# The first feed-forward layer from its third group on: seven half-size products in place of eight, and the loop's down weights rounded on VectorE

## The reference, cut to what matters

```python
h = rms_norm(x, g_pre_ffn)
f = jnp.square(jax.nn.relu(h @ w_ff1)) @ w_ff2      # 1024 -> 4096 -> 1024
return x + rms_norm(f, g_post_ffn)
```

## Time and profile before

| | |
|---|---|
| median of 3 runs | 1717.76 us (1717.62 to 1719.08) |
| profiled execution | 1716.92 us, span 1715.0 us |
| TensorE busy | 1698.2 us, 99% of the span |
| VectorE busy | 1104.3 us, 64% |
| ScalarE busy | 783.1 us, 46% |
| GpSimd busy | 585.6 us, 34% |
| mean granted TensorE clock | 0.998 |
| DMA | 162.61 MB, mean 95 GB/s |

### The profile page before, as it was taken

One profiled execution on the slowest core, in us unless ns is written; L12 is line 12 of the kernel. 1 busy time (PEld: TensorE's weight loads), 2 busy tenths in 40 slices (PEclk: granted clock), 3 DMA queues, 4 the chain that ended last, 5 costly groups with the idle time before them and its releaser, 6 DMA issues.

```text
span 1715.0 us, 27666 instructions
## 1 busy us (share of the span) xinstructions
PE 1698.2 (99%) x9346; PEld 1459.2 (85%) x9346; DVE 1104.3 (64%) x1973; ACT 783.1 (46%) x1323; POOL 585.6 (34%) x289
## 2 busy tenths in 40 slices
PE   9999999999999999999999999999999999999998
PEld 7877778888888788889999998888888879999997
DVE  5655565333333587688787695566675588688684
ACT  5666543222222433653443354565655453353354
POOL 3232325444445378241210203442523440220221
PEclk9999999999999999999999999999999999999999
DMA  7542213222222242233322333231212233342331
GB/s 197 119 99 85 74 59 126 94 93 96 98 98 87 74 129 87 74 111 99 112 94 90 110 99 111 74 99 49 86 61 74 75 100 96 101 132 74 98 111 50
DMA packets 153712, 162.61 MB, mean 95 GB/s; under 512 B 10627, under 2 KB 114679, under 8 KB 153631
## 3 DMA queue, kind: packets, MB, share of 16 engines
q1 hardware_dynamic: 149167, 158.66, 30.1%
q10 hardware_dynamic: 4464, 2.89, 0.5%
HBM read 157.84 MB, written 3.67 MB: 94 GB/s over the span
## 4 chain that ended last, share of the span: by engine, by line
PE 92%; DVE 4%; ACT 2%; issue 1%; DMA 0%; SPq 0%; DVEq 0%; ACTq 0%
PE ps L1675 49%; PE ps L2080 21%; PE ps L2105 10%; PE ps L1696 2%; PE ps L2187 1%; PE ps L2023 1%; PE ps L1704 1%; PE ps L1894 1%; PE ps L1913 1%; DVE ps L2715 1%; PE ps L1800 0%; PE ps L1806 0%; PE ps L2220 0%; PE ps L1877 0%; DMA lnmult<-const_lnmult 0%
## 5 line engine op out<-in xcount | busy, mean ns | idle before, releaser
L835 POOL TENSOR_TENSOR wlo<-raw,whi 128x1024 fp32r<-128x1024 f32 x92 | 224.8, 2451 | 339.3 <-ACT whi L952 324.0
L1675 PE MATMUL ps<-h_hi,wlo 128*128 128x512 f32 x800 | 323.0, 404 | 6.5 <-DVE gate L2814 5.7
L1675 PE MATMUL ps<-h_hi,whi 128*128 128x512 f32 x800 | 313.1, 391 | 0.0
L1675 PE MATMUL ps<-h_lo,whi 128*128 128x512 f32 x800 | 312.9, 391 | 0.0
L952 ACT ACTIVATE whi<-raw 128x1024 fp32r<-128x1024 f32 x170 | 176.5, 1055 | 251.1 <-PE ps L1675 241.7
L842 POOL TENSOR_TENSOR wlo<-raw,whi 128x1024 fp32r<-128x1024 f32 x60 | 146.9, 2464 | 293.3 <-ACT whi L952 170.2
L1675 PE MATMUL ps<-m_hi,wlo 128*128 128x512 f32 x544 | 214.9, 395 | 0.0
L1675 PE MATMUL ps<-m_hi,whi 128*128 128x512 f32 x544 | 211.9, 390 | 0.0
L1675 PE MATMUL ps<-m_lo,whi 128*128 128x512 f32 x544 | 211.8, 389 | 0.0
L1675 PEld LDWEIGHTS ps<-h_hi,wlo 128*128 128x128 f32 x800 | 150.7, 188 | 38.5 <-issue 8.1
L1675 PEld LDWEIGHTS ps<-h_hi,whi 128*128 128x128 f32 x800 | 150.6, 188 | 33.0
(11 more groups left out here) (411 smaller groups left out, 3938.9 us busy)
## 6 DMA issues: line engine op xcount, KB each, us to landing
raw<-in_ffn_w SPq DMA_DIRECT2D x264, 256.0 KB, 2.9
raw<-in_w_ff SPq DMA_DIRECT2D x128, 256.0 KB, 2.7
raw<-in_hg_w_in SPq DMA_DIRECT2D x64, 256.0 KB, 3.0
raw<-in_w_in SPq DMA_DIRECT2D x40, 256.0 KB, 5.2
raw<-in_cp_w_in SPq DMA_DIRECT2D x24, 256.0 KB, 2.8
raw<-in_w_out SPq DMA_DIRECT2D x16, 256.0 KB, 3.0
raw<-in_cp_w_out SPq DMA_DIRECT2D x16, 256.0 KB, 3.0
raw<-in_hg_w_out SPq DMA_DIRECT2D x16, 256.0 KB, 2.9
```

Of the source, the lines that this page charges most:

```text
L835: pool.tensor_tensor(wlo[:, u % RING, :, :], raw[:, u % RING, :, :], whi[:, u % RING, :, :].bitcast(F32), ALU.subtract).then_inc(unit_lo, 1)
L1675: mm = pe.matmul(ps[:, b, :], wt[:, s, a, m * P:(m + 1) * P], xt[:, kts[a], :], start=starts and a == 0 and i == 0, stop=last)
```

## The change

In the first feed-forward layer, groups 0 and 1 stay as they are. Groups 2 to 7 are done as twelve blocks of 256 columns, each seven products of half size (12 matmuls of 256 columns each). TensorE's order is now up 0, norm, up 1, down 0, down 1, block 0, then five turns of (block, block, down), then block 11 and down 7. The weight sums and the low parts of the forms are VectorE's, as in the gated layers; so are now the low parts of the loop's down weights (`ffn_down_low`), 8 tiles of 128 x 512 a turn. GpSimd does nothing from unit 15 of the layer to unit 60. The four token sums are made once, between up 1 and the first `acc` copies. The buffers `hid` and `hid2` are now `sq` and `ss`. Counters of the later layers are shifted to match. The forms have 11 slots (the gated layers 12).

The core of the diff; on VectorE:

```diff
+            def ffn_token_sums():
+                dve.wait_ge(tokens_made, 4)
+                for k in range(4):
+                    dve.scalar_tensor_tensor(out=f3[:, k, :], in0=xT[:, 4 + k, HALF:], scalar=col("g_pre_ffn", 4 + k),
+                                             in1=f1[:, k, HALF:], op0=ALU.mult, op1=ALU.subtract).then_inc(tokens_made, 1)
+                dve.wait_ge(tokens_made, 8)
+                dve.tensor_tensor(f1[:, :, HALF:], f1[:, :, HALF:], f1[:, :, 0:HALF], ALU.subtract).then_inc(tokens_made, 1)
+                dve.wait_ge(tokens_made, 9)
+                for k in range(4):
+                    dve.scalar_tensor_tensor(out=f2[:, k, :], in0=xT[:, 4 + k, HALF:], scalar=col("g_pre_ffn", 4 + k),
+                                             in1=f1[:, k, HALF:], op0=ALU.mult, op1=ALU.subtract).then_inc(tokens_made, 1)
+                dve.wait_ge(tokens_made, 13)
+                for k in range(4):
+                    dve.scalar_tensor_tensor(out=f1[:, k, 0:HALF], in0=xT[:, 4 + k, 0:HALF], scalar=col("g_pre_ffn", 4 + k),
+                                             in1=f2[:, k, :], op0=ALU.mult, op1=ALU.subtract).then_inc(tokens_made, 1)
...
+            def ffn_hidden(j, t, i=None):
+                dve.tensor_tensor(hid2[:, :], ffn_kept(j)[:, t, :], ffn_kept(j)[:, t, :], ALU.mult).then_inc(hid_ready, 1)
+                dve.wait_ge(hid_hi, at(i, 4, 8 + 2 * j + t + 1))
+                dve.tensor_tensor(m_lo[:, 2 * (j % 2) + t, :], hid2[:, :], m_hi[:, 2 * (j % 2) + t, :].bitcast(F32),
+                                  ALU.subtract).then_inc(hid_lo, 1)
...
+            def ffn_forms(y, i, after):
+                ffn_sum(y, 1, i)
+                ffn_sum(y, 2, i)
+                ffn_low(y, 0, i)
+                ffn_sum(y, 3, i)
+                ffn_low(y, 1, i)
+                after(1)
+                ffn_low(y, 2, i)
+                ffn_sum(y, 4, i)
+                after(2)
+                ffn_low(y, 3, i)
+                after(3)
+                ffn_low(y, 4, i)
+                after(4)
+                ffn_low(y, 5, i)
+                after(5)
+                ffn_low(y, 6, i)
+            def ffn_during(x, y, i=None):
+                ffn_forms(y, i, lambda n: {1: ffn_u2, 2: ffn_u3, 3: ffn_p5, 5: ffn_c11}[n](x, i) if n != 4 else None)
+                ffn_c12(x, i)
             ffn_up(0, 0, 0)
             ffn_up(1, 0, 1)
-            ffn_down(0, first=True)
-            with dve.Fori(0, FFN_GROUPS // 2 - 1) as i:
-                ffn_up(i * 2 + 2, i * 2 + 1, 0)
-                ffn_down(i * 2 + 1)
-                ffn_up(i * 2 + 3, i * 2 + 2, 1)
-                ffn_down(i * 2 + 2)
+            ffn_token_sums()
+            ffn_down(0, first=True, halves=(0,))
+            for f in F_TOKEN_ORDER:
+                ffn_token_lo(f)
+            ffn_down(0, first=True, halves=(1,))
+            dve.wait_ge(tokens_lo, F_TOKENS)
+            ffn_forms(0, None, lambda n: ffn_down(1, halves=(0,)) if n == 4 else None)
+            ffn_down(1, halves=(1,))
+            ffn_during(0, 1)
+            ffn_c21(0)
+            with dve.Fori(0, F_TURNS) as i:
+                ffn_hidden(0, 0, i)
+                ffn_during(1, 2, i)
+                ffn_c21(1, i)
+                ffn_hidden(0, 1, i)
+                ffn_down_low(0, i)
+                ffn_hidden(1, 0, i)
+                ffn_down_low(1, i)
+                ffn_u2(2, i)
+                ffn_hidden(1, 1, i)
+                ffn_down_low(2, i)
+                ffn_u3(2, i)
+                ffn_p5(2, i)
+                ffn_down_low(3, i)
+                ffn_c11(2, i)
+                ffn_c12(2, i)
+                ffn_c21(2, i)
+                for d in range(4, 8):
+                    ffn_down_low(d, i)
+                ffn_forms(3, i, lambda n: ffn_down(i + 2, halves=(0,)) if n == 4 else None)
+                ffn_down(i + 2, halves=(1,))
+...
```

On GpSimd, ScalarE and TensorE:

```diff
-            lo_parts(0, U_CPIN - 8)
+            lo_parts(0, U_FFN + 16)
...
-            for j in range(8):
-                lo_part(U_CPIN - 8 + j)
-                if j % 2 == 0:
-                    table(1, j // 2)
+            for j in range(4):
+                lo_part(U_FFN + F_LATER + j)
+                if j == 0:
+                    pool.wait_ge(filled[ffn_bank(F_LAST, "c21")], ffn_nth(F_LAST, None, "c21"))
+                    pool.wait_ge(hid_lo, 4 * FFN_GROUPS)
+                table(1, j)
...
+            ffn_up(4, 1, 0, 1)
+            for k in range(4):
+                act.activation(f1[:, k, :], xT[:, k, :], ACT.Copy, scale=vecs[:, c:c + 1]).then_inc(tokens_made, 1)
+            for j in range(2):
+                split(U_FFN, 8 + j)
+            ffn_token_hi(2)
+            ffn_token_hi(3)
+            split(U_FFN, 10)
+            ffn_token_hi(1)
+            split(U_FFN, 11)
+            ffn_token_hi(6)
...
+            ffn_up(4, 0)
+            ffn_down(8, 0, 0)
+            ffn_down(12, 1, 1)
+            ffn_products(0, 0)
+            with pe.Fori(0, F_TURNS) as i:
+                ffn_products(1, 2, i)
+                ffn_products(2, 1, i)
+                ffn_turn_down(i)
+            ffn_products(F_LAST, 2)
+            ffn_down(F_LATER, FFN_GROUPS - 1, 0)
```

More of the change, by code:

```diff
@@ new lines, in _, with ffn_products @@
+            ffn_down(12, 1, 1)
+            def ffn_products(j, slots_before, i=None):
+                for f in range(FORMS):
+                    s = ffn_form_slot(ffn_slot(j) + f)
+                    b = ffn_bank(j, TAGS[f])
+                    x_hi, x_lo = ffn_rounded(f)
+                    pe.wait_ge(form_lo, at(i, 2 * FORMS, FORMS * j + f + 1))
+                    if j == 0 and f in (1, 6):
+                        pe.wait_ge(tokens_lo, 3 if f == 1 else 4)
+                    pe.wait_ge(drained[b], ffn_nth(j, i, TAGS[f]) - 1)
+                    for k in range(4):
+                        for p, (wt, xt) in enumerate(((ffn_lo_slot(s), x_hi), (ffn_hi_slot(s), x_lo), (ffn_hi_slot(s), x_hi))):
+                            begins, ends = k == 0 and p == 0, k == 3 and p == 2
+                            mm = pe.matmul(ps[:, b, 0:HALF], wt[:, k * P:(k + 1) * P], xt[:, k, :],
+                                           start=begins and TAGS[f] != "c11",
+                                           stop=ends, skip_group_check=TAGS[f] == "c11")
+                            if begins and f == 0 and j == 0:
+                                mm.then_inc(unit_begun, 1)
+                            elif begins and not (f == 1 and j == 0):
+                                mm.then_inc(form_used, 1 if f else slots_before)
+                            if ends:
+                                mm.then_inc(filled[b], 1)
@@ new lines, in ffn_turn_down @@
+            def ffn_turn_down(i):
+                for q in range(4):
+                    h, p = q // 2, q % 2
+                    s = [ffn_form_slot(F_DOWN + 2 * q + a) for a in range(2)]
+                    pe.wait_ge(down_lo, at(i, 8, 2 * q + 2))
+                    begun = False
+                    for a, m in [(a, m) for m in range(4) for a in range(2)] if p else [(a, m) for a in range(2) for m in range(4)]:
+                        kt = 2 * p + a
+                        if m == 0:
+                            pe.wait_ge(hid_lo, at(i, 4, 8 + kt + 1))
+                        if p == 0 and a == 0:
+                            pe.wait_ge(drained[4 + m], before("ffndown", ("d", h, m), i + 2))
+                        for r, (wt, xt) in enumerate(((ffn_lo_slot(s[a]), m_hi), (ffn_hi_slot(s[a]), m_lo), (ffn_hi_slot(s[a]), m_hi))):
+                            last = p == 1 and a == 1 and r == 2
+                            mm = pe.matmul(ps[:, 4 + m, :], wt[:, m * P:(m + 1) * P], xt[:, kt, :],
+                                           start=kt == 0 and r == 0, stop=last)
+                            if not begun:
+                                mm.then_inc(form_used, 2 if q else 1)
+                                begun = True
+                            if last:
+                                mm.then_inc(filled[4 + m], 1)
@@ L2627, in ffn_up, with ffn_down @@
                     parts(m)
-            def ffn_down(g, first=False, last=False):
-                for h in range(2):
+            def ffn_down(g, first=False, last=False, halves=(0, 1)):
+                for h in halves:
                     for m in range(4):
```

370 lines of the change are left out of this document (320 added, 50 removed).

## The result

The changed kernel takes 1727.6 us in the median of five executions (1727.25 to 1728.92), the kernel before 1717.76: a ratio of 1.0057, 95% interval 1.0046 to 1.0069. It is slower by some 10 us. The forecast was 1723.0, 5.2 us slower, with a range of 1716 to 1728: the side is right, the size was half, and the time lies only 0.4 us inside the top of the range.

A forecast was written before the change was run, and what follows sets the result against it. TensorE, 99% busy, was taken to bound the kernel. Terms -9.6 + 8.0 + 1.6 + 2.0 + 2.8 + 0.4 = +5.2 us on the profiled 1716.92, plus 0.84 to the median, gave 1723.0 us, range 1716 to 1728.

The forecast's parts named there:

- Products, -9.6: TensorE's matmuls in the layer: 1008 of 256 columns replace 576 of 512, saving 9.6 us.
- Token sums, +8.0: Down 0: TensorE waits 8.0 us for VectorE's token sums, lengthened by three GpSimd subtractions; between 1.4 and 9.
- rivals with none or two falling in: Down 0, GpSimd subtractions among the token sums: none, 1714.8 us, chance 0.12; two, 1720.7 us, chance 0.2.
- Clock behind it, +1.6: Behind down 0's wait: TensorE runs at 1.2 GHz for 8 matmuls, costing 1.6 us; between 0 and 3.
- Loop, +2.0: Five turns: VectorE frees two banks late, 0.3 us a turn and 0.75 in the first; 0 to 5.
- Last down part, +3.2: Down 7: 2.8 us waiting for unit 61's low part behind a table piece, 0.4 for an `acc` copy; 0 to 5.
- VectorE becomes the bound in the loop: Rival, loop: ScalarE's round trips cost 1 us a turn more, five turns add 5, 1728 us; chance 0.12.

The follow-up runs named there:

- small_lows: Changed kernel with GpSimd's low parts of hidden units 10, 11 and 12 made over 64 of 512 columns: 1718.87 us, ratio 1.0007.
- hold_tail: Changed kernel with 12 small unused products on TensorE ahead of unit 61 in the last down part: 1726.52 us, ratio 1.0047.
- tables_last: Changed kernel with GpSimd's low parts of units 60 to 63 made ahead of its four table pieces: 1721.98 us, ratio 1.0026.
- loop_order: Changed kernel with VectorE's u3, p5 and half 0's accumulator copies made earlier in each loop turn: 1726.09 us, ratio 1.0043.
- gpsimd_downs: Changed kernel with the loop's eight down-weight low parts a turn given back from VectorE to GpSimd: 1751.57 us, ratio 1.0191.
- copies_first: Changed kernel with VectorE copying half 0 of down 0 out of its banks before making the token sums: 1718.26 us, ratio 1.0004.
- hold_clock: Changed kernel with 24 small unused products on TensorE ahead of unit 10's product in down 0: 1728.33 us, ratio 1.0057.
- hold_full: Changed kernel with 34 small unused products on TensorE ahead of unit 10's product in down 0: 1725.11 us, ratio 1.0040.

## Why the prediction was right or wrong

- **Products, -9.6.** Right: a block takes 10.08 us (341.07 to 351.15). The estimate by the formula of the Trainium skill (TensorE: Matmul & The Clock Gate, Back-to-back issue gap), 14.2 us saved, is not borne out.
- **Token sums, +8.0.** Right, measured 7.7, with three subtractions among them; small_lows shows the cause. The wait came at the predicted place (287.85 forecast, 288.04 + 0.23 measured) and ended at 296.00 (295.9 forecast). The rivals with none or two falling in are out. What the Trainium skill says (SBUF — State Buffer, Who interferes with whom), that such a VectorE instruction and a GpSimd one that reads SBUF shut each other out, agrees with 3.8 against 1.67 us for the same four sums.
- **Clock behind it, +1.6.** The effect was right, and 2.35 were measured, inside the bound of 3: 11 slow matmuls in place of the 8 of the earlier trace rows. But the size is no fixed one. Behind the same wait of 7.6 us, in kernels whose edits all lie later, the same stretch lost 2.25 us in hold_tail, 2.08 in tables_last, 1.62 in loop_order and 1.54 in gpsimd_downs, with 7 to 10 slow matmuls. So 1.6 lies within what one execution differs from another by; what sets the number of slow matmuls stays open.
- **Loop, +2.0.** The places were right, the term half of the measured 4.1. VectorE's time was: `ffn_u3(2)` was to be done after 18.9 us and is after 18.97 (402.73 + 0.42 - 384.18). What the step left out is that TensorE does not start at that moment: from the end of that sum to the next matmul are 0.14 us, and the start behind it comes after 0.19 us, not 0.12. So 0.3 a turn became 0.72, and 0.75 in the first turn became 1.18.
- **Last down part, +3.2.** The wait for unit 61 was right, 2.8 forecast and measured, and tables_last shows its cause. The step that failed is that the clock's fall stood only among the bounds (+1.6). It fell, and cost 1.9 us with the slow starts. The wait on `acc` (0.4 forecast) hangs on it: it is 0.8 or 0.9 in the four traces whose clock fell here, and none of the other traces shows one, though GpSimd holds the sum of squares up there too (2.03 us long in copies_first).
- **Sum.** Forecast +5.2, measured +10.1 in the layer. The missing 4.9 us are 2.1 in the loop, 1.9 for the second fall, 0.75 for the first, 0.4 for `acc`, less 0.3 for a wait that was 7.7. Each wait was found; what was missed is what TensorE loses beyond the end of the wait. That all of it falls on one side is why the time stands at the edge of the range, which held with 0.4 us to spare; by that much it was luck.
- The rival "VectorE becomes the bound in the loop" named a time close to the measured one (1728), but for another reason: no turn is bound by VectorE, and in loop_order a few steps moved ahead take all but one short wait away.

## What to carry to other kernels

Where one engine is at 99%, ask of every instruction list what frees its next bank, and put that ahead of work that is only needed later: here three moves in order, with no work less, turned +10 us into -7. Price a new wait of some us with the lower clock behind it (1.5 to 2.4 us here), and a short one with some 0.2 us over what the two engines' steps give. Two engines that shut each other out of SBUF must be planned as one: taking work off the busier one and giving it to the other can cost more than it frees (24 us here).

## What the runs showed that was not expected

- **The same wait, with and without a fall of the clock.** The last down part's wait is 2.62 or 2.63 us in seven traces. Behind it the clock fell to 1.2 GHz in four (the changed kernel, hold_clock, loop_order, gpsimd_downs) and held in three (copies_first, small_lows, hold_full). The four are those in which the clock had also fallen in down 0, some 280 us earlier. In hold_full, which differs from hold_clock only in ten small products there, the second fall went with the first. That the first causes the second is not shown: an edit at down 0 also shifts by some us when the last wait comes. For a sum, a wait of 2.6 us has to be priced with and without the fall: 2.3 us here, with the `acc` wait that comes with it.
- **A shorter wait in another place also brought it.** In gpsimd_downs 1.2 GHz follows on waits of 2.0 us in the loop (granted 0.52), while 1.66 us had left the clock alone, and so did 1.73 in small_lows.
- **The clock need not fall during the wait.** In hold_clock it is still 2.4 GHz for the first five matmuls behind it, in the changed kernel's last down part for the first three; the slow ones follow. Behind down 0's 7.6 us, and behind the last wait in loop_order, the first matmul is already slow.
- Each small product of 128 x 128 counts as two instructions in the trace, which take 0.23 us together (34 in 7.75 us), where 0.31 had been reckoned.
